# The next head's preparation dealt over all steps of an attention head, and two banks for its rough scores

## The reference

```python
q = (c_q @ w_q_b).reshape(B, L, N_HEADS, QK_HEAD_DIM)
kv = (c_kv @ w_kv_b).reshape(B, L, N_HEADS, QK_NOPE_DIM + V_HEAD_DIM)
k_nope, v = kv[..., :QK_NOPE_DIM], kv[..., QK_NOPE_DIM:]
...
q = rmsnorm_2(q, g_qn)
k = rmsnorm_2(k, g_kn)
...                       # rotate the last 32 of q and k
s = jnp.where(valid, s, MASK_VALUE)          # causal
p = jax.nn.softmax(s, axis=-1).astype(v.dtype)
outs.append(jnp.einsum('bhqk,bkhd->bqhd', p, v[:, :kend]))
```

## Time and profile before

| | us |
|---|---|
| median of 3 runs | 3507.73 |
| lowest, highest | 3506.89, 3511.37 |
| the profiled execution, its own time | 3510.98 |
| its span from first to last instruction | 3509.2 |
| TensorE matmul busy | 3118.4 (89%) |
| VectorE busy | 1437.4 (41%) |
| ScalarE busy | 699.0 (20%) |
| GpSimd busy | 1081.3 (31%) |

### The profile page before, as it was taken

One profiled execution on the slowest core, in us unless ns is written; L12 is line 12 of the kernel. 1 busy time (PEld: TensorE's weight loads), 2 busy tenths in 40 slices (PEclk: granted clock), 3 DMA queues, 4 the chain that ended last, 5 costly groups with the idle time before them and its releaser, 6 DMA issues.

```text
span 3509.2 us, 41107 instructions
## 1 busy us (share of the span) xinstructions
PE 3118.4 (89%) x16352; PEld 2721.2 (78%) x16352; DVE 1437.4 (41%) x1730; ACT 699.0 (20%) x1239; POOL 1081.3 (31%) x1335
## 2 busy tenths in 40 slices
PE   6975677899999994999997999888999998899899
PEld 4754555777777773999996777788999997677789
DVE  4677455322222226500114555553620113555561
ACT  2132310000000002001112454400000111444410
POOL 2532022344444441533432100133433432111122
PEclk9987789999999997999998999999999998899999
DMA  2101011111111111112112000142112112000041
GB/s 99 48 25 33 1 69 41 48 45 45 48 48 47 43 48 67 49 49 95 45 43 79 13 7 13 37 153 97 38 48 97 43 49 79 13 13 13 14 170 72
DMA packets 46206, 182.50 MB, mean 52 GB/s; under 512 B 5745, under 2 KB 5873, under 8 KB 45553
## 3 DMA queue, kind: packets, MB, share of 16 engines
q1 hardware_dynamic: 31248, 113.19, 10.2%
q10 hardware_dynamic: 14816, 67.28, 5.0%
HBM read 150.06 MB, written 30.39 MB: 51 GB/s over the span
## 4 chain that ended last, share of the span: by engine, by line
PE 75%; DVE 16%; issue 3%; ACT 3%; POOL 1%; DMA 1%; DVEq 0%; POOLq 0%; ACTq 0%; SPq 0%
PE acc L411 56%; PE aux L778 3%; PE acc L666 3%; PE acc L757 3%; DVE act_lo L1362 2%; PE acc L715 1%; DVE residual L1427 1%; DVE small L1789 1%; PE acc L732 1%; POOL w_lo L341 1%; DVE act_hi L1361 1%; PE acc L651 1%; DVE work L1378 1%; PE acc L679 1%; PE acc L689 1%
## 5 line engine op out<-in xcount | busy, mean ns | idle before, releaser
L411 PE MATMUL acc<-act_hi,w_hi 128*128 128x348 f32 (+1 forms) x3104 | 772.8, 350 | 112.1 <-DVE act_lo L1362 40.5
L341 POOL TENSOR_TENSOR w_lo<-w_raw,w_hi 128x256 fp32r<-128x256 f32 (+1 forms) x924 | 827.5, 926 | 17.2
L411 PE MATMUL acc<-act_lo,w_hi 128*128 128x348 f32 (+1 forms) x3104 | 763.7, 346 | 0.0
L411 PE MATMUL acc<-act_hi,w_lo 128*128 128x348 f32 (+1 forms) x3104 | 763.2, 346 | 0.0
L411 PEld LDWEIGHTS acc<-act_hi,w_hi 128*128 128x128 f32 x3104 | 547.6, 191 | 172.8 <-issue 65.6
L411 PEld LDWEIGHTS acc<-act_lo,w_hi 128*128 128x128 f32 x3104 | 550.0, 190 | 43.9
L411 PEld LDWEIGHTS acc<-act_hi,w_lo 128*128 128x128 f32 x3104 | 547.0, 190 | 42.2
L361 POOL TENSOR_TENSOR small<-shape_consts 128x1 f32<-128x1 f32 x192 | 40.3, 210 | 1606.7 <-PE acc L411 1606.7
L411 PE MATMUL acc<-ff_split,w_hi 128*128 128x512 f32 (+1 forms) x1408 | 351.9, 375 | 12.1 <-DVE ff_split L1362 12.1
L1579 DVE TENSOR_TENSOR residual<-acc,residual 128x1024 f32<-128x1024 f32 (+1 forms) x88 | 108.2, 1229 | 482.0 <-PE acc L411 482.0
L411 PEld LDWEIGHTS acc<-ff_split,w_hi 128*128 128x128 f32 x1408 | 254.3, 188 | 60.0 <-DVE ff_split L1362 16.6
(11 more groups left out here) (228 smaller groups left out, 3385.6 us busy)
## 6 DMA issues: line engine op xcount, KB each, us to landing
w_raw<-in_wstream SPq DMA_DIRECT2D x215, 512.0 KB, 3.5
spill_x<-residual ACTq DMA_DIRECT2D x2, 4176.0 KB, 12.2
spill_m<-residual ACTq DMA_DIRECT2D x2, 4176.0 KB, 12.6
spill_g<-work ACTq DMA_DIRECT2D x2, 4176.0 KB, 12.4
residual<-spill_m ACTq DMA_DIRECT2D x16, 522.0 KB, 5.8
work<-spill_g ACTq DMA_DIRECT2D x16, 522.0 KB, 8.7
residual<-spill_x ACTq DMA_DIRECT2D x16, 522.0 KB, 4.5
residual<-in_xT ACTq DMA_DIRECT2D x8, 512.0 KB, 9.9
```

Of the source, the lines that this page charges most:

```text
L341: ins = nc.gpsimd.tensor_tensor(Wl[:, s, c0:c0 + w], Wraw[:, s, c0:c0 + w], Wh[:, s, c0:c0 + w].bitcast(F32), ALU.subtract)
L411: ins = nc.tensor.matmul(acc[0:m, s, p, 0:w], wt[:, ws, w0 + j * m:w0 + j * m + m], x[:, k, p * w:p * w + w], start=(first and t == 0), st ...
```

## The change

Nothing of the computation changes, and no instruction is added or removed, but for the place of each in its engine's program.

- *Banks.* The keys and values are projected into `acc_n`, the bank of the sums. The bank of `acc_k` becomes a second bank for rough tiles: the 15 rough tiles and 3 turned maxima of a head are counted through, and take the two banks in turn. `r_free` is kept for each bank.
- *Steps.* A piece begins in steps 0, 5 and 10 in place of 0, 4 and 8, so that the preparation runs over all 15 steps. In each group of five steps TensorE does the key and value part, the three query parts (with the key sum in the second of them and the value transposes in the third), and then the query sum, beside the work of head h. The norms of the last piece move into the first two steps of the next head (`key_norm(h, 2)`, `query_norm(h, 2)`, `query_scale(h, 2)`). The rough tiles of piece 2 stand in steps 2 to 5 in place of 1 to 4, the others in steps 7 to 9 and 12 to 14; step 12 has two.
- *Within a step* the rough tiles come ahead of the projection, and the value copies on ScalarE come last.

```diff
+        ROUGH_USES = []
+        for pc in range(NQP):
+            ROUGH_USES += [t for t in ROUGH if t[0] // 3 == pc] + [pc]
...
+        def rough_bank(i, p):
...
-        acc_q, acc_k, acc_n = (acc[:, 0, i, :] for i in range(3))
-        acc_s, acc_r = (acc[:, 1, 0, :], acc[:, 1, 1, :]), acc[:, 1, 2, :]
+        acc_q, acc_n = acc[:, 0, 0, :], acc[:, 0, 2, :]
+        acc_s, acc_r = (acc[:, 1, 0, :], acc[:, 1, 1, :]), (acc[:, 0, 1, :], acc[:, 1, 2, :])
...
-                    if k > 1:
-                        pe.wait_ge(sems["k_free"], k - 1)
+                    if n_free[0] is not None:
+                        pe.wait_ge(*n_free[0])
...
-                            ins = nc.tensor.matmul(acc_k[:, 0:w], wt[:, w_head[0], (6 + j) * P:(7 + j) * P],
+                            ins = nc.tensor.matmul(acc_n[:, 0:w], wt[:, w_head[0], (6 + j) * P:(7 + j) * P],
...
+                    n_free[0] = (sems["k_free"], k)
...
+                    bank = rough_bank(i, p)
+                    if r_free[bank] is not None:
+                        pe.wait_ge(*r_free[bank])
...
+                    r_free[bank] = (sems["rough_max"], rough_no(l, h, i, p))
...
-                    pe.wait_ge(*r_free[0])
+                    bank = turn_bank(pc)
+                    if r_free[bank] is not None:
+                        pe.wait_ge(*r_free[bank])
                     if pc:
                         pe.wait_ge(sems["max_ready"], 2 * (l * MH + h) + pc)
+                    else:
+                        pe.wait_ge(sems["rough_max"], rough_no(l, h, 2, 0))
...
                     for n in range(NB):
                         if h >= 0:
                             scores(h, n)
+                            if n in (2, 3, 4):
+                                rough_scores(h, 4 + n, 0)
+                            if n == 5:
+                                rough_scores(h, 8, 2)
+                        if more:
+                            if n in (7, 8, 9):
+                                rough_scores(g, n - 7, 0)
+                            if n == 12:
+                                rough_scores(g, 3, 0)
+                            if n == 13:
+                                rough_scores(g, 4, 1)
+                            if n == 14:
+                                rough_scores(g, 5, 1)
+                            if n in (0, 5, 10):
+                                key_value_part(g, n // 5)
+                            if n % 5 in (1, 2, 3):
+                                query_part(g, n // 5, n % 5 - 1)
+                            if n in (2, 7, 12):
+                                key_sum(g, n // 5)
+                            if n in (3, 8, 13):
+                                turn_values(g, n // 5)
+                            if n in (4, 9, 14):
+                                query_sum(g, n // 5)
+                            if n == 10:
+                                turn_maxima(g, 0)
+                            if n in (12, 13):
+                                rough_scores(g, n - 8, 0)
+                        if h >= 0:
                             if n == 0:
                                 turn_maxima(h, 1)
-                            if n in (1, 2, 3):
-                                rough_scores(h, 5 + n, 0)
-                            if n == 4:
-                                rough_scores(h, 8, 2)
+                            if n in (2, 3, 4):
+                                rough_scores(h, 4 + n, 1)
                             if n == 5:
                                 turn_maxima(h, 2)
-                        if more:
-                            if n in (8, 9, 10):
-                                rough_scores(g, n - 8, 0)
-                            if n == 11:
-                                turn_maxima(g, 0)
-                            if n in (12, 13, 14):
-                                rough_scores(g, n - 9, 0)
-                            if n in (0, 4, 8):
-                                key_value_part(g, n // 4)
-                            elif n < 12:
-                                query_part(g, n // 4, n % 4 - 1)
-                            if n in (3, 7, 11):
-                                key_sum(g, n // 4)
-                            if n in (4, 8, 12):
-                                query_sum(g, n // 4 - 1)
-                            if n in (6, 10, 13):
-                                turn_values(g, (n - 6) // 3)
-                            if n in (13, 14):
-                                rough_scores(g, n - 9, 1)
-                        if h >= 0 and n in (1, 2, 3):
-                            rough_scores(h, 5 + n, 1)
-                        if h >= 0 and n >= 2:
-                            weigh_values(h, n - 2)
-                        if h >= 1 and n < 2:
-                            weigh_values(h - 1, NB - 2 + n)
+                            if n >= 2:
+                                weigh_values(h, n - 2)
+                            elif h >= 1:
+                                weigh_values(h - 1, NB - 2 + n)
                 weigh_values(MH - 1, NB - 2)
                 weigh_values(MH - 1, NB - 1)
                 pe.wait_ge(sems["p_in"], block_no(l, MH - 1, NB - 1))
                 pe.wait_ge(sems["k_free"], wave(l, MH - 1, NQP - 1))
...
                     g = h + 1
                     more = g < MH
                     for n in range(NB):
+                        if h >= 0 and n == 1:
+                            maximum_row(h, 1)
+                        if h >= 0 and n == 6:
+                            maximum_row(h, 2)
+                        if more and n in (5, 10):
+                            query_scale(g, n // 5 - 1)
+                        if h >= 0 and n == 0:
+                            query_scale(h, 2)
                         if h >= 0:
                             exponents(h, n)
-                            if n == 0:
-                                maximum_row(h, 1)
                             if n == 2 and h >= 1:
                                 inverse_sums(h - 1, 2)
                             if n == 4:
                                 inverse_sums(h, 0)
-                            if n == 5:
-                                maximum_row(h, 2)
                             if n == 9:
                                 inverse_sums(h, 1)
-                            if n == 1 and not more:
+                            if n == 3 and not more:
                                 act.wait_ge(sems["k_lo"], wave(l, h, NQP - 1))
                                 act.wait_ge(sems["q_lo"], wave(l, h, NQP - 1))
                                 for j in range(4, KC):
...
                         if more:
                             if n == 11:
                                 maximum_row(g, 0)
-                            if n in (4, 8, 12):
-                                key_scale(g, n // 4 - 1)
-                            if n in (0, 4, 8):
-                                key_value_evict(g, n // 4)
-                            if n in (5, 9, 13):
-                                query_scale(g, n // 4 - 1)
-                            if n in (7, 11, 14):
-                                values_in(g, (n - 7) // 3)
-                            if n in (3, 7, 11):
-                                query_squares(g, n // 4)
+                            if n in (0, 5, 10):
+                                key_value_evict(g, n // 5)
+                            if n in (3, 8, 13):
+                                key_scale(g, n // 5)
+                                query_squares(g, n // 5)
+                            if n in (4, 9, 14):
+                                values_in(g, n // 5)
                 inverse_sums(MH - 1, 2)
                 by_signal(0)
                 for j in range(4):
...
                     more = g < MH
                     for n in range(NB):
                         if h >= 0:
+                            if n == 0:
+                                key_norm(h, 2)
+                            if n == 1:
+                                query_norm(h, 2)
+                        if more and n == 4:
+                            query_table(g, 0)
+                        if h >= 0:
+                            if n in (2, 3, 4):
+                                maximum(h, 4 + n, 0)
                             if n == 3 and h >= 1:
                                 head_out(h - 1, 2)
-                            if n in (1, 2, 3):
-                                maximum(h, 5 + n, 0)
-                                maximum(h, 5 + n, 1)
-                            if n == 4:
+                            if n in (2, 3, 4):
+                                maximum(h, 4 + n, 1)
+                            if n == 5:
                                 maximum(h, 8, 2)
                                 maxima_of(2)
-                            if n == 5:
+                            if n == 6:
```

(39 more changed lines are left out.)

33 lines of the change are left out of this document (17 added, 16 removed).

## The result

The changed kernel takes 3451.03 us (median, 3447.57 to 3455.5) against 3507.31 us of the kernel before: ratio 0.984, 95% interval 0.9823 to 0.9857. The profiled execution took 3447.57 us, 3445.8 from first to last instruction: 63.4 less than before's span of 3509.2.

The account below looks back on a forecast made before the run. TensorE was taken as the bound: a period is 45.5 us of matmuls and stops plus the clock's share. Periods -9.6, prologues -10, last heads -5.6, clock 0 make -25 us: 3483 us, forecast 3470 to 3500, range 3460 to 3508.

Parts of the forecast that it names:

- The first rival: Full clock all through the head loops: 25.4 us more saved, 3457 us; chance 0.14.
- my own sign of being wrong: Wrong if rough tiles wait for casts in each head, or the periods' mean clock leaves 0.92 to 0.96.
- stops that come, steps 4, 9, 14, as the profile counts: Query sum waits for ScalarE's copy of the turned values: near 1.75, 1.6 and 0.65 us a head.
- steady head at full clock: In each steady head 5.5 us of TensorE stops go and 4.7 come: -0.8 us.
- 12 periods without the clock: The steady head's -0.8 us over 12 periods of the head loops: -9.6 us.
- prologues: Preparation of head 0 in each layer: -5 us a layer, -10 together.
- last heads with the period ahead: Last head of each layer -2 us, the full period ahead of it -0.8: -5.6 for two layers.
- clock in the periods: Low-clock spells in the 12 periods cost 25 us as before: 0, between -25 and +43.
- the rough tiles' stops: Steps 12 to 14: two banks end the waits for reductions, 0.62 and 0.90 us, 1.5 together a head.
- the 2 us for the clock: Prologue: stops of 2.2 and 1.3 us lower the clock, so 2 of the 7 us gained are taken back.
- the third rival: Late norms: VectorE 1 us late at steps 7 and 12, +25 us, so 3508, no change; chance 0.12.
- the keys' new bank: Key projection's wait for the query scale's logarithm is covered by last values and next scores (1.1 us): no cost.

Follow-up runs that it names:

- the run with one bank: The changed kernel with its new order, but every rough tile and turned row in one bank: 3464.93 us, ratio 0.9876 against before.
- the run with filler: The kernel before, with 11 matmuls a head added ahead of the score tiles of steps 13 and 14, which then overwrite them: 3495.03 us, ratio 0.9965.
- the run with four small copies: The changed kernel with four small ScalarE copies ahead of the values' copy in steps 4 and 9: 3502.86 us, ratio 0.9988.
- the last filler: The changed kernel with the values' copy ahead of the exponentials, plus 38, 12 and 9 unread matmuls in each layer's prologue: 3398.54 us, ratio 0.9691.

## Why the prediction was wrong

**The step that failed is the clock.** "I expect the clock to fall behind one of them in most heads and behind both in some ... 1.25 spells of 1.7 is 2.1 a head, 25 us, as before. 0". There is no spell in any of the twelve periods, and this term is -25.6. The first rival, with a chance of 0.14, was what happened, and my own sign of being wrong came with it: the mean clock of the periods left 0.92 to 0.96. I reasoned from the length of the longest stop. What the rows had shown is that before's clock fell with stops of 0.6 and 0.62 ahead of it and within one of 0.90, among mostly narrow matmuls; the run with one bank shows that the new order takes this away by itself, and the run with filler that most of the stops can stay and the clock be full. The run with four small copies shows how near the other side was: 0.8 us more in a stop and each head has its spell, with a total of 3502.86. So my argument was not without ground, but its price was put on stops that lie on the harmless side. Where between 1.77 and 2.60 us that side ends, and why 2.64 in step 9 is still harmless, no run settles. Nor is the other side of it settled: what about before's narrow stretch lowered the clock stays open, since TensorE was busy longer in it than around after's stop (2.35 against 1.63 of 3.40 us).

The Trainium skill, "TensorE: Matmul & The Clock Gate", A second HAM failure mode, says that short idling between groups of matmuls makes the clock swing if it is frequent enough, and does not say how frequent. Before swings with six stops and 4.46 us a head; after, with three stops and 3.94 us, does not. So what I had drawn from it, that a change which keeps these stops keeps the swings, did not hold here.

**The sum by its other terms.** Forecast and measured, in us:

| term | forecast | measured |
|---|---|---|
| stops that come, steps 4, 9, 14, as the profile counts | 1.75, 1.6, 0.65 | 1.77, 1.68, 0.49 |
| steady head at full clock | -0.8 | -1.16 |
| 12 periods without the clock | -9.6 | -15.3 |
| prologues | -10 | -12.8 |
| last heads with the period ahead | -5.6 | -8.4 |
| clock in the periods | 0 | -25.6 |
| sum | -25 | -62.1 |

- The stops that come were right to 0.2 us, and so was their mechanism. By the profile's count stops fall from 4.46 to 3.94, and from six places to three, 0.17 each: 1.03 in all, near the 1.16 seen. I had kept 0.15 for the transposes and 0.16 too much in step 14. Why the rough tiles' stops go was wrong: I gave their 1.5 us a head to the two banks, and with one bank in the new order they are gone too (periods of 44.46 against 44.32).
- Prologue: the first rough tile waits 1.88 us for the query's cast (L728 behind L1792), 2.2 forecast. With the 2 us for the clock the forecast has the next projection at 2993, 46.75 us from the prologue's start; it is 46.88. The difference in the table is the 1.36 of turned maxima, which lie in the prologue in before and behind it in after. But the parts were not right, and that they cancel is luck: from that tile on I had 11.7 us of matmuls, 3.7 of stops and 2 for the clock, and the row has TensorE busy for 15.70 of 17.67 us, at a clock of 0.84.

```profile
2942.31:2959.98 17.67, 15.70 (x75) 12.46 (x75) 9.84 (x21) 7.04 (x17) 2.10 (x4) 0.84 0.00 0
```

- Last heads: 5.1 and 3.3 in place of 2.8 each. Part of it is the clock again, 0.94 and 0.98 over that stretch in before and 1.00 in after; at the price of a period in the earlier trace rows (2.9 us for a clock of 0.92) I estimate it at some 4 us of the 8.4. Without it the last heads give less than forecast: stops of 0.8 and 0.7 us behind VectorE stay, where I had near none.
- The norms came in time. In the steady heads of after no rough tile waits for a cast: the third rival's place shows nothing, and the margin was enough.
- The two parts of the change: in before's order two banks lose 49 us, since the keys' projection collides with the key scale; the order has to come with the bank. The forecast costed the keys' new bank at nothing, which holds only in the new order. The order alone keeps the clock and gives 39.7 us of the 40.9 in the periods.

## What to carry to other kernels

Price the clock by stretches, not by the longest stop: where the trace shows 1.2 GHz, look at what TensorE did just ahead of it, and ask whether the new order leaves such a stretch anywhere. Neither the longest stop nor TensorE's busy time sorted the heads here, so a run has to confirm it. Such a stretch can be cured by moving real work into it (here 25.6 us) and even by work that nobody reads (12 us, ratio 0.9965). When a bank is shared anew, put whatever frees it first in the queue of the engine that does it: one copy moved ahead of an exponential was worth another 48 us, and the last filler 5 more, to 3398.5 us against 3507.

## What was not expected of the hardware

- At a clock of 1.00 with stops of 1.77 and 1.68 us in each head, it is steady through the head loops of both layers; with 2.60 or 2.73 in step 4 it falls in every one, for 3.4 us; with 4.53 and 4.44 (4.66 and 4.57 in the next head) for 6.8 us at each.
- Of two stops nearly alike in one head (2.60 and 2.51 us, 2.73 and 2.64 in the next) the same one lowers the clock each time. What tells them apart stayed open.
- The clock fell behind 3.40 us in which TensorE was busy for 2.35, and did not where it was busy for 1.63.
- 11 unread matmuls in each head made the kernel before faster by 0.35%.
